# Two roots and a table load moved to the end of the sample stage on ScalarE, in a hybrid state-space and attention layer

## The reference

```python
def layer_output(x, gate, y_ssd, o_br, g_raw, z_a, att_norm_g, w_out):
    ...
    o = jnp.sum(gates * o_br, axis=2).reshape(B, T, ATT_WIDTH)
    y_att = rms_norm(o * jax.nn.silu(z_a), att_norm_g)
    mix = jnp.concatenate([y_ssd, y_att], axis=-1) @ w_out
    return x + gate[:, None] * mix
```

## Time and profile before

| | |
|---|---|
| median of 3 runs | 896.88 us (896.66 to 896.91) |
| profiled execution | 893.61 us, span of its instructions 891.7 us |
| busy, share of the span | PE 93%, PEld 61%, DVE 59%, ACT 40%, POOL 28% |
| mean granted TensorE clock | 0.987 |
| output stage, 536 to 892 us | about 356 us |

### The profile page before, as it was taken

One profiled execution on the slowest core, in us unless ns is written; L12 is line 12 of the kernel. 1 busy time (PEld: TensorE's weight loads), 2 busy tenths in 40 slices (PEclk: granted clock), 3 DMA queues, 4 the chain that ended last, 5 costly groups with the idle time before them and its releaser, 6 DMA issues. The chain is left out here.

```text
span 891.7 us, 20080 instructions
## 1 busy us (share of the span) xinstructions
PE 828.3 (93%) x8505; PEld 542.3 (61%) x8505; DVE 528.3 (59%) x1099; ACT 359.7 (40%) x735; POOL 253.9 (28%) x212
## 2 busy tenths in 40 slices
PE   3999999999999999998999997779988989799996
PEld 2447998877788665666455555435646464554553
DVE  2146752377788645548424546886866867667711
ACT  4041002011222354455232336864765666444532
POOL 2049879350000142345111100146110130302121
PEclk9999999999999999999999999998999999999999
DMA  9952255535020100304754235510020010202021
GB/s 304 344 178 102 89 202 214 209 144 189 1 73 1 29 1 0 95 1 153 284 170 137 76 129 169 163 37 2 15 70 29 13 59 9 71 3 72 15 97 48
DMA packets 45411, 89.06 MB, mean 100 GB/s; under 512 B 4388, under 2 KB 26076, under 8 KB 43210
## 3 DMA queue, kind: packets, MB, share of 16 engines
q1 hardware_dynamic: 38202, 54.94, 19.0%
q0 software_dynamic: 6080, 31.79, 10.2%
q10 hardware_dynamic: 1040, 1.05, 0.4%
HBM read 75.49 MB, written 16.40 MB: 103 GB/s over the span
## 5 line engine op out<-in xcount | busy, mean ns | idle before, releaser
L2184 PE MATMUL PS<-W,hT 128*128 128x512 f32 x256 | 113.0, 594 | 0.3 <-DVE W L1800 0.3
L1970 DVE CUSTOM_DVE_ANT_0 PS<-PS,consts 128x640 f32<-128x640 f32 (+5 forms) x96 | 77.4, 838 | 33.7 <-PE PS L2602 33.2
L1098 POOL TENSOR_TENSOR Q<-Q,U 128x512 f32<-128x512 f32 x16 | 20.3, 1267 | 247.1 <-DVE U L2004 247.1
L2184 PEld LDWEIGHTS PS<-W,hT 128*128 128x128 f32 x256 | 47.9, 190 | 55.9 <-issue 54.8
L1412 ACT ACTIVATE hT<-PS,small 128x128 f32<-128x128 f32 (+7 forms) x64 | 46.9, 742 | 53.1 <-DVE small L1970 51.0
L2569 PE MATMUL PS<-U,Y 128*128 128x512 f32 x128 | 62.0, 618 | 0.8 <-ACT Y L1426 0.8
L2569 PE MATMUL PS<-U,Q 128*128 128x512 f32 x128 | 59.0, 599 | 0.0
L1412 ACT ACTIVATE T<-PS,small 128x640 f32<-128x640 f32 (+4 forms) x64 | 41.7, 661 | 30.4 <-DVE small L1970 30.1
L1986 DVE STREAM_TRANSPOSE hT<-hT 128x1024 f32<-128x1024 f32 (+6 forms) x29 | 42.4, 1482 | 1.9 <-ACT hT L1412 1.8
L2569 PEld LDWEIGHTS PS<-U,Q 128*128 128x128 f32 x128 | 23.5, 190 | 30.3 <-issue 30.3
L2569 PEld LDWEIGHTS PS<-U,Y 128*128 128x128 f32 x128 | 23.2, 194 | 28.3 <-issue 26.0
(11 more groups left out here) (542 smaller groups left out, 1862.3 us busy)
## 6 DMA issues: line engine op xcount, KB each, us to landing
W<-in_w_in SPq DMA_DIRECT2D x4, 2048.0 KB, 7.9
W<-in_w_ada SPq DMA_DIRECT2D x7, 1024.0 KB, 16.4
U<-in_x_prompt SPq DMA_DIRECT2D x8, 512.0 KB, 11.1
W<-in_w_ada SPq DMA_DIRECT2D x2, 2048.0 KB
U<-in_state_win_kv POOLq DMA_DIRECT2D x8, 512.0 KB
W<-in_x_prompt SPq DMA_DIRECT2D x8, 512.0 KB, 3.8
out_y_prompt<-W SPq DMA_DIRECT2D x8, 512.0 KB, 3.3
out_new_win_sample<-in_state_win_kv POOLq DMA_DIRECT2D x1, 4032.0 KB, 24.0
```

The lines of the kernel that those rows point to most:

```text
L1098: nc.gpsimd.tensor_tensor(Q3[:, i, :], Q3[:, i, :], spare, ALU.add).then_inc(s_added, 1)
L1970: ins = nc.vector.tensor_tensor_reduce(x, x, strip(u), 1.0, -NEG, ALU.add, ALU.min, sneg_m[u % 2][:, m:m + 1])
L2184: ins = nc.tensor.matmul(bank(z_bank(u)), hT3[:, k, i * P:(i + 1) * P], w, start=(k == 0), stop=(k == KT8 - 1))
```

## The change

The roots leave the step SAMPLE and stand behind the last gate of the sample stage, ahead of the wait for its last sum (`s_smp_sum`), with one exponential of one column behind them, whose value isn't used.

```diff
                 z_silu(Z_AMID[p])
 
+            act.wait_ge(s_ysq, 9)
+            yssq = ssq.rearrange("p (i s) -> p i s", s=2)[:, :, 0:1]
+            for a, b, n in ((0, TT, P), (TT, TT + 1, SR)):
+                act.activation(yssq[0:n, a:b], yssq[0:n, a:b], ACT.Sqrt, scale=1.0 / SW, bias=eps2[0:n]).then_inc(s_yroot, 1)
+            act.activation(half_sums[:, 0:1], eps2, ACT.Exp)
             act.wait_ge(s_smp_sum, 4)
             for (what, u), again in zip(STEPS, AGAIN):
                 tile = MIX[u] if what in OUTPUT else None
                 r = rows(tile) if what in OUTPUT else None
-                if what == "SAMPLE":
-                    act.wait_ge(s_ysq, 9)
-                    q = ssq.rearrange("p (i s) -> p i s", s=2)[:, :, 0:1]
-                    for a, b, n in ((0, TT, P), (TT, TT + 1, SR)):
-                        act.activation(q[0:n, a:b], q[0:n, a:b], ACT.Sqrt, scale=1.0 / SW, bias=eps2[0:n]).then_inc(s_yroot, 1)
                 if what == "GATE":
```

## The result

| | before | after |
|---|---|---|
| median, 6 executions each | 896.77 us (895.68 to 897.05) | 892.11 us (888.45 to 894.10) |
| ratio | | 0.9944, 95% interval 0.9920 to 0.9967 |
| profiled execution | 893.61 us, clock 0.987 | 894.10 us, clock 0.979 |

What follows compares the result with a forecast made beforehand. TensorE is busy most of the span, but in two places all engines wait behind one ScalarE instruction. Some 0.6 sooner by 561, about 2.0 by 576, carried to the end: 896.88 - 2.0 = 894.9 us; range 892.8 to 897.3.

Steps and rivals of the forecast that it cites:

- What a measurement can tell: Whole kernel: a change of 0.2%, 1.8 us, is about what a measurement can tell from no change.
- Put in at 536.59: ScalarE after the last sample gate: loads, roots and exponential take 3.4 within 3.90 of idle time, costing nothing.
- Taken out at 542.91: Table load ahead of the first softmax step: 1.28 removed, worth some 0.6 by 561.
- Taken out at 561.73: ScalarE in the step SAMPLE: load, roots, load, 3.1 removed; the seventh softmax step starts 1.45 sooner, at 563.4.
- What then is late: the values step behind s9: TensorE's 128 matmuls behind the last scores: they end at 570.5, and the copy comes 2.1 sooner, at 571.15.
- I take the clock to stay up there: TensorE at 569 to 572: full clock instead of 0.50; if it falls as before, the sum is -1.1.
- The pause to 575.98 is not carried along, or VectorE binds: Rival in the second place, at TensorE's pause without a releaser: only -0.6, 896.3; chance 0.12.
- The drain around a load: Rival at the inserted loads: ScalarE runs empty around each, a load costs 2.6, net +0.8, 897.7; chance 0.05.

Runs made afterwards that it cites:

- overrun kernel: Changed kernel with two more table loads and two more unused one-column operations behind the roots; mean 897.99 +- 0.9 us.
- the table only: Kernel before with only the unused exponential added behind the last gate, roots left in the step SAMPLE; mean 892.92 +- 0.9 us, ratio 1.0008.
- before, third: Kernel before, no edit, third profile and set of 12 executions; mean 894.58 +- 1.0 us, ratio 0.9993 to the kernel before beside it.
- before, again: Kernel before, no edit, profiled and timed once more, 12 executions; mean 896.52 +- 0.9 us, ratio 1.0045 to the kernel before beside it.

## Why the prediction was wrong

- *What a measurement can tell.* What failed for the total: "a change of 0.2%, about what a measurement of this kernel can tell from no change". The three runs shown spanned 0.25 us; over many, single executions of one kernel spread over 8 to 10, and sets of 12 have means 2 apart. -4.66 is 2.66 from the forecast. The whole study puts the change at -0.6 +- 0.6, or -1.2 +- 0.4 at an equal clock, which is nearer to nothing than the forecast and far from the first measurement. So two things are separate. The measured 892.11 lies under the range, but the medians of the two later sets (895.36 and 893.66) lie in it, so that miss is mostly one of which executions were timed. The forecast of -2.0 itself was too large by a step of its path.
- *Put in at 536.59.* Right: 3.30 in an idle time of 3.9, 0.58 left (forecast 3.4 and 0.5). The overrun kernel shows the price of more: x0 2.33 late where 2.4 was expected.
- *Taken out at 542.91.* Right, step for step: x0 1.29 sooner (1.30), x1 0.30 (0.3), x2 0.58 and the first copy 0.60 at best (0.6 to 0.7), the values step of the second place 0.59 at equal falls of the clock.
- *Taken out at 561.73.* x6 was to be at 23.1 from s0 (563.4 less 540.32). It was at 23.8 to 24.1: the long fall of the clock in the first place, which the prediction did not price, cost 0.7 to 1.0. At equal falls x6 came 1.41 sooner (25.48 and 24.07), as the forecast of 1.45 had it.
- *"What then is late: the values step behind s9."* **This is the step that failed on the path.** The values step needs two turnings by VectorE, the second of which ended at 570.04; s9 ended at 570.10. The prediction took it as waiting for TensorE's own order, because its row had no idle time, and names no input from VectorE. The kernel says otherwise (the selected branch of the second tile has two units, each with its turning, and the step waits for the last of them):

```python
                        pe.wait_ge(s_pturned, TURNED["TURNP", LAST_TURN[i, k]])
```

The tie of 0.06 was partly the clock's: s9 took 1.46 at 0.50, and with 0.92 it would have ended 0.5 before the turning, as it does with the table only (0.55). VectorE itself came only 0.6 sooner, so the step could start at 569.5 at best and not at 568.1. Forecast 2.1 sooner at the copy; measured 0.39 at equal falls (33.97 and 33.58), and over three profiles each 33.6 to 33.9 from s0 against 32.9 to 34.0, which is no gain.

- *"I take the clock to stay up there."* Wrong in all three profiles after: it is at 0.50 from 26.7, 29.5 or 28.8 from s0 on, and the values step's start to the copy takes 3.4 to 3.8 instead of the 3.2 before and the 3.05 of the forecast (568.1 to 571.15).
- *The rivals.* "The pause to 575.98 is not carried along, or VectorE binds", -0.6, had 0.12. Its second half is what the runs show, though it named no step at which VectorE binds; its first half isn't borne out, as the pause moves with the values step. The drain around a load doesn't show: in the profile after a load again starts 0.02 behind the instruction before it, and one operation of one column sits between two loads 1.5 apart (542.42 and 543.93 of the overrun kernel), where the Trainium skill (ScalarE: Activation LUTs, What ACT_TABLE_LOAD costs) would have about 2.66 for the switch alone. The measurement decides.

## What to carry to other kernels

When an engine's row shows no idle time, look up every input of that step, not only the one before it in its queue: two chains may end within 0.1 us, and then shortening the one that isn't last gives nothing, while lengthening it by 3.0 cost 3.1 here. A table load moved into idle time is worth what the next operand's wait leaves of it, here 0.3 of 1.28 at the next step and 0.6 at the end of the place. And before a forecast of 0.2% is compared with a measurement, run the unchanged kernel twice: here it differed from itself by 2 us between sets of 12, and by 4 between a set and the 35 executions beside it.

## What was unexpected of the hardware

The granted clock falls at other places in each execution of one program: of three profiles of the kernel before, two lose 6.8 us at 0.50 around 63 us behind s0 and one keeps 1.00 there; six of the fourteen profiles (among them before, third, and after, but neither before nor before, again) also have one that starts near 18 us from the start of the program and lasts 6.8 to 10.2, hundreds of microseconds ahead of every edit. The same time at 0.50 costs much or little by place. With 6.8 us of it around 63 the path from s0 was 3.1 longer (351.4 against 348.3, with five stretches at 0.50 in the one and four in the other), of 3.4 that half speed can cost. In the first place 3.4 us more at 0.50 cost about 1.0 (x6 at 25.48 against 24.51), of 1.7.
